# The buffers and transfers of the expert weights in a two-layer mixture-of-experts block

## What is computed

```python
D_MODEL, N_EXPERTS, TOP_K, EXPERT_DIM = 1024, 64, 8, 256

def _moe_routed(h, idx, wts, wg, wu, wd):
    ...
    def step(acc, blk):
        tok, w, e = blk
        xb = h_pad[tok]
        y = (jax.nn.silu(xb @ wg[e]) * (xb @ wu[e])) @ wd[e]
        return acc.at[tok].add(y * w[:, None].astype(y.dtype)), None
```

## Time and profile before

| | us |
|---|---|
| median of 3 runs | 3108.76 |
| lowest and highest | 3108.38, 3108.87 |
| the profiled execution | 3109.16 |
| its span, first to last instruction | 3107.3 |

### The profile page before, as it was taken

How to read it: one execution, slowest core, us unless ns; L and a number is a source line. 1 busy time by engine, 2 the same in 40 slices (tenths; PEclk the granted TensorE clock), 3 DMA queues, 4 the chain that set the end, 5 groups by cost and what they waited for, 6 DMA issues and landing times. The chain is left out here.

```text
span 3107.3 us, 44283 instructions
## 1 busy us (share of the span) xinstructions
PE 2711.0 (87%) x13505; PEld 1375.2 (44%) x13506; DVE 1126.3 (36%) x3283; ACT 575.0 (19%) x1306; POOL 389.7 (13%) x312
## 2 busy tenths in 40 slices
PE   5998989896969999999997588999977988999894
PEld 3555655654523333333332275666643333333331
DVE  2443452523323333333332643451433322223223
ACT  2222331311001111111111331331210111111111
POOL 0000001001012222222221200001010212122121
PEclk7999999996989999999998799999978999999997
DMA  6111213014177998999994502102134899998993
GB/s 250 55 72 41 84 40 120 14 42 175 48 288 237 363 324 266 317 310 325 328 354 128 200 1 85 68 28 107 35 146 188 336 371 379 365 390 283 380 329 100
DMA packets 109039, 619.21 MB, mean 199 GB/s; under 512 B 22800, under 2 KB 27152, under 8 KB 69264
## 3 DMA queue, kind: packets, MB, share of 16 engines
q1 hardware_dynamic: 75248, 530.30, 43.7%
q0 software_dynamic: 33696, 87.63, 11.6%
HBM read 578.84 MB, written 77.99 MB: 211 GB/s over the span
## 5 line engine op out<-in xcount | busy, mean ns | idle before, releaser
L1439 PE MATMUL ps<-wgu,xT 128*64 128x512 f32 x3584 | 820.2, 611 | 62.2 <-DMA wgu<-in_exp_gu 54.2
L1439 PEld LDWEIGHTS ps<-wgu,xT 128*64 128x64 f32 x3584 | 258.8, 140 | 529.0 <-issue 527.1
L1449 PE MATMUL ps<-wd,hiddenT 128*64 128x512 f32 x1824 | 421.2, 604 | 12.6 <-issue 11.5
L530 PE MATMUL ps<-w_in,hT 128*128 128x512 f32 (+3 forms) x1152 | 385.2, 493 | 14.5 <-PEq L484 3.8
L1375 POOL DMA_INDIRECT ffn_rows<-Y,six x114 | 182.5, 1601 | 1162.9 <-issue 779.0
L1598 DVE TENSOR_TENSOR hidden<-silu,ps 128x256 f32<-128x256 f32 x112 | 47.2, 421 | 737.0 <-ACT silu L1538 737.0
L530 PEld LDWEIGHTS ps<-w_in,hT 128*128 128x128 f32 x1152 | 205.2, 195 | 190.2 <-issue 183.2
L1449 PEld LDWEIGHTS ps<-wd,hiddenT 128*64 128x64 f32 x1824 | 128.3, 138 | 225.6 <-issue 225.6
L1538 ACT ACTIVATE silu<-ps 128x256 f32<-128x256 f32 x112 | 43.0, 384 | 831.6 <-PE ps L1439 831.6
L1592 DVE TENSOR_SCALAR Y<-ps,wc 128x512 f32<-128x512 f32 x114 | 85.6, 751 | 202.7 <-PE ps L1449 202.7
L1424 PE MATMUL ps<-cst,X 128*128 128x128 f32 x912 | 126.3, 282 | 34.9 <-DMA X<-h_rows,gix 19.1
(11 more groups left out here) (455 smaller groups left out, 2898.7 us busy)
## 6 DMA issues: line engine op xcount, KB each, us to landing
wgu<-in_exp_gu SPq DMA_DIRECT2D x128, 2048.0 KB, 13.1
wd<-in_exp_d SPq DMA_DIRECT2D x128, 1024.0 KB, 10.9
ada_start<-in_ada_w SPq DMA_DIRECT2D x8, 1024.0 KB, 13.2
w_in<-in_w_in SPq DMA_DIRECT2D x4, 2048.0 KB, 9.8
w_in<-in_w_out SPq DMA_DIRECT2D x4, 2048.0 KB, 11.9
aw_0A<-in_ada_w SPq DMA_DIRECT2D x6, 1024.0 KB, 4.8
aw_0B<-in_ada_w SPq DMA_DIRECT2D x6, 1024.0 KB, 5.0
aw_0C<-in_ada_w SPq DMA_DIRECT2D x6, 1024.0 KB, 4.8
```

What stands on the lines that cost most here:

```text
L530: last = pe.matmul(pp[i % 2][:, c0:c1], hT[:, k, i * P:(i + 1) * P], wg[g % 2][:, k, c0:c1], start=(k == 0), stop=(k == KD - 1))
L1439: last = pe.matmul(ps[h * HB:(h + 1) * HB, 0, :], xT[:, k, h * HB:(h + 1) * HB], wgu[w[h]][:, k, :], start=(k == 0), stop=(k == KD - 1))
L1449: last = pe.matmul(ps[h * HB:(h + 1) * HB, 1 + c, :], G[:, f, h * HB:(h + 1) * HB], wd[w[h]][:, f, c * 512:(c + 1) * 512], start=(f == 0), ...
```

## The change

The two tiles of a buffer become one, `wexp`, of 128 x 6144 numbers (3 MB); `wgu` and `wd` are now views into it. The weights lie in memory accordingly, the gate, up and down weights of an expert side by side (`exp_w`, made on the host before the launch, as the two arrays were). An expert is loaded with one transfer of 3 MB, which raises one semaphore, `weights_landed`; the gate/up and the down products both wait for it. SP's loop is one loop over the experts 4 to 63, with one wait each, on the count of down products. The products, their order and the passes stay as they are. The diff, cut to its core:

```diff
-        self.wgu = [sb(f"wgu0_{l}", [P, KD, 2 * FD], scope=scope)]
-        self.wd = [sb(f"wd0_{l}", [P, 2, D], scope=scope)]
+        self.w = [sb(f"wexp0_{l}", [P, KD * 2 * FD + 2 * D], scope=scope)]
...
-    eng.dma_start(ex.wgu[e][:, :, :].rearrange("p k n -> p (k n)"), v.t["exp_gu"][l, e]).then_inc(v.S(f"gate_up_landed{e}_{l}").sem, 16)
-    eng.dma_start(ex.wd[e][:, :, :].rearrange("p k n -> p (k n)"), v.t["exp_d"][l, e]).then_inc(v.S(f"down_landed{e}_{l}").sem, 16)
+    eng.dma_start(ex.w[e][:, :], v.t["exp_w"][l, e]).then_inc(v.S(f"weights_landed{e}_{l}").sem, 16)
...
-                def load_gate_up(w, e, free):
-                    sp.wait_ge(gate_up, free + CREDIT)
...
-                def load_down(w, e, free):
-                    sp.wait_ge(down, free + CREDIT)
...
-                with sp.Fori(0, E // NB - 2) as group:
+                with sp.Fori(1, E // NB) as group:
                     for w in range(NB):
-                        e = group * NB + (NB + 1 + w)
-                        load_gate_up((w + 1) % NB, e, free_after(e))
-                        load_down(w, e - 1, free_after(e - 1))
...
+                        e = group * NB + w
+                        free = sp.value_load(table[0:1, bass.ds(e + T_FREE, 1)], min_val=0, max_val=pairs)
+
+                        sp.wait_ge(down, free + CREDIT)
+                        sp.dma_start(ex.w[w][:, :], v.t["exp_w"][l][bass.ds(e, 1)].rearrange("a p n -> (a p) n")).then_inc(w_landed[w], 16)
...
-                        pe.wait_ge(w_gu[w[h]], landed[h])
+                        pe.wait_ge(w_landed[w[h]], landed[h])
...
-                        pe.wait_ge(w_d[w[h]], landed[h])
+                        pe.wait_ge(w_landed[w[h]], landed[h])
```

More of the change, by code:

```diff
@@ L1281, in sem @@
         return S(f"{n}_{l}").sem
-    w_gu, w_d = [sem(f"gate_up_landed{w}") for w in range(NB)], [sem(f"down_landed{w}") for w in range(NB)]
+    w_landed = [sem(f"weights_landed{w}") for w in range(NB)]
     listed, indexed, index, gathered = sem("slots_marked"), sem("slots_summed"), sem("index_ready"), [sem("gathered0"), sem("gathered1")]
@@ L1297, in experts @@
         for w in range(1, NB):
-            ex.wgu.append(sb(f"wgu{w}", [P, KD, 2 * FD]))
-            ex.wd.append(sb(f"wd{w}", [P, 2, D]))
-        wgu, wd, X, Y = ex.wgu, ex.wd, ex.X, ex.Y
+            ex.w.append(sb(f"wexp{w}", [P, KD * 2 * FD + 2 * D]))
+        X, Y = ex.X, ex.Y
+        wgu = [w[:, 0:KD * 2 * FD].rearrange("p (k n) -> p k n", k=KD) for w in ex.w]
+        wd = [w[:, KD * 2 * FD:].rearrange("p (k n) -> p k n", k=2) for w in ex.w]
         SG, HID, G = sb("silu", [P, FD]), sb("hidden", [P, FD]), sb("hiddenT", [P, 2, P])
@@ L1331, in _ @@
             def _(sp):
-                def load_gate_up(w, e, free):
-                    sp.wait_ge(gate_up, free + CREDIT)
-                    sp.dma_start(wgu[w][:, :, :].rearrange("p k n -> p (k n)"),
-                                 v.t["exp_gu"][l][bass.ds(e, 1)].rearrange("a p n -> (a p) n")).then_inc(w_gu[w], 16)
-                def load_down(w, e, free):
-                    sp.wait_ge(down, free + CREDIT)
-                    sp.dma_start(wd[w][:, :, :].rearrange("p k n -> p (k n)"),
-                                 v.t["exp_d"][l][bass.ds(e, 1)].rearrange("a p n -> (a p) n")).then_inc(w_d[w], 16)
@@ L1342, in free_after @@
-                def free_after(e):
-                    return sp.value_load(table[0:1, bass.ds(e + T_FREE, 1)], min_val=0, max_val=pairs)
                 for e in range(1, NB):
                     load_expert(v, sp, l, e, ex)
-                sp.wait_ge(gate_up, free_after(NB) + CREDIT)
-                sp.dma_start(wgu[0][:, :, :].rearrange("p k n -> p (k n)"), v.t["exp_gu"][l, NB]).then_inc(w_gu[0], 16)
-                with sp.Fori(0, E // NB - 2) as group:
+                with sp.Fori(1, E // NB) as group:
@@ L1359, in _ @@
-                sp.wait_ge(down, free_after(E - 1) + CREDIT)
-                sp.dma_start(wd[(E - 1) % NB][:, :, :].rearrange("p k n -> p (k n)"), v.t["exp_d"][l, E - 1]).then_inc(w_d[(E - 1) % NB], 16)
+                        e = group * NB + w
+                        free = sp.value_load(table[0:1, bass.ds(e + T_FREE, 1)], min_val=0, max_val=pairs)
+                        sp.wait_ge(down, free + CREDIT)
+                        sp.dma_start(ex.w[w][:, :], v.t["exp_w"][l][bass.ds(e, 1)].rearrange("a p n -> (a p) n")).then_inc(w_landed[w], 16)
@@ L1799, in layout @@
         "router_w": f["router_w"], "sh_g": f["sh_w_gate"], "sh_u": f["sh_w_up"], "sh_d": f["sh_w_down"],
-        "exp_gu": gu.reshape(L, E, P, KD * 2 * FD), "exp_d": ed.reshape(L, E, P, 2 * D),
+        "exp_w": np.concatenate([gu.reshape(L, E, P, KD * 2 * FD), ed.reshape(L, E, P, 2 * D)], axis=3),
     }
```

## The result

The changed kernel takes **3458.3 us** (median, 3454.9 to 3461.6) against 3108.8 before: 1.112 times the time, 95% interval 1.111 to 1.114. The forecast was 3480 with a range of 3400 to 3565. The profiled execution took 3454.9 us, span 3453.1, against 3109.2 and the earlier trace rows: +345.8 us of span, which is what follows by terms.

What follows compares the result with a forecast made beforehand. TensorE bounds the first expert loop, TensorE and the DMA queue in turns the second. Layer 1 stalls 342 + 8, layer 0 24 + 12, replaced waits -54, clock +40: 3109 + 372 = 3481, say 3480 us, range 3400 to 3565.

Steps and rivals of the forecast that it cites:

- table of distances: Both expert loops: passes from a buffer's last use to its next; distance 2 for 30 layer 1 reloads, 2 in layer 0.
- many waits under 1.5 us: First expert loop: perhaps many short TensorE waits for weights behind gate/up products, at reloads three passes apart.
- stall of distance 2: Gate/up products two passes after the buffer's last use: transfer fully exposed, landing 12.2 us, stall 12.0 us each.
- double ones: Five layer 1 passes needing two experts of distance 2: the second adds 8.4 us, 20.4 each.
- Pass 30: Layer 1: experts 43 and 44 leave behind one down and are both needed, 20.6 us against 12.4: 8 us.
- edge of distance 3 in layer 0: 24 layer 0 loads with 12.4 us from issue to need, against 12.2 to land: 0.5 us each, 12 together.
- waits that go: Second loop: the 12 existing waits for gate/up weights fall on passes that now stall longer and are replaced, -54 us.
- The clock: Gate/up products behind each stall run partly at 1.2 GHz, 2.1 us a stall over 28 stalls: +40 us.
- Waits for gathered rows: TensorE's waits for gathered rows may shrink as the queue is emptier: 0 to -10 us, taken 0.
- fewer, larger transfers feed the queue better: Rival: the DMA queue is the bound and one transfer per expert saves completions, so not slower: 3036 us; 2 in 100.
- The clock came back: Rival denied here: TensorE stays at 1.2 GHz in stalled passes, 12.5 us each in place of 2.1: 3760 us; 4 in 100.
- none took 16: Rival: the exposed transfer beside gather and scatter packets lands in 16 us, adding 180 us: 3660 us; 4 in 100.

Runs made afterwards that it cites:

- order_after: The changed kernel with experts reordered within groups of eight on the host, so 15 layer 1 reloads have distance 2 in place of 30: 3308.0 us.
- m5_after: The changed kernel with five weight buffers in place of four: 3235.4 us, 1.041 times the kernel before.
- late_two_both: The changed kernel without merging: two transfers of 2 and 1 MB, both released by the down count, gate/up products waiting for both: 3472.1 us.
- merged_8k: The changed kernel with 32 bytes of padding behind each 8 KB of a buffer row, cutting the 3 MB transfer into 8 KB pieces: 3502.9 us.

## Why the prediction was right

- **Where TensorE waits**: the table of distances named all 28 passes and no other; order_after and m5_after moved the waits as the table moves. Only the many waits under 1.5 us that layer 0 might have shown are absent, see the edge below.
- **A stall of distance 2**: forecast 12.0 us, from a landing of 12.2; measured 11.3 on average over the 22 single ones (10.7 to 12.0). The double ones: 20.4 forecast, 19.8 to 20.4 measured. Pass 30: 8 forecast, 7.8 measured. Together 374 forecast, 356 measured. The size was taken from the five quickest pairs of reloads in the trace; late_two_both shows what such a pair costs here, 13.5 us, and that the merged load is faster than it, 11.8. So 12.2 was too low for a pair, and that the merging would help the landing was left out of the sum. That the two nearly cancel is luck. The 9.2 us of the Trainium skill's fit (page DMA: Bandwidth & Descriptors, Anatomy of one DMA) is below every landing of 3 MB of weights in the changed kernel (10.7 us at the least).
- **The edge of distance 3 in layer 0**: forecast 12 us, measured 0. The term that was off is the landing again: 11.8 us is inside the 12.4 of cover. That the edge is there is shown by late_two_both and merged_8k, which land in 13.5 us and wait 17 times in layer 0, 15 of them at distance 3.
- **The waits that go**, -54, and down products that never wait for weights: as forecast.
- **The clock**: forecast +40, at 2.1 us a stall; measured +37. The gate/up products behind the 28 waits took 8.4 to 10.0 us, 9.1 on average, in place of 7.09.
- **Waits for gathered rows**: forecast 0 to -10, with 0 taken; measured +25. The step that failed is "may shrink as the queue is emptier": the queue is emptier on average, but the packets beside the gather's are longer, and merged_8k brings the waits back to 11.7. The quicker landing took 30 us off the forecast (18 in the stalls, 12 at the edge) and small waits of the kind "issue" another 14, for which the forecast had no term and no run shows a reason; the gathered rows put 25 on. That the sum stood within 22 us of the result owes something to luck, the 356 us of waits for weights do not.
- **The rivals**: "fewer, larger transfers feed the queue better" was right in kind and wrong in size: 14 us of 3472. It ends far from 3036, since at distance 2 the load is issued too late for the queue to matter: pass 2 waits for its own transfer from the issue on. The Trainium skill's advice to coalesce into one large transfer (the same page, Rules for kernel authors) is given there for many small transfers; here, with 1 and 2 MB, it was worth those 14 us. Its advice to issue early and wait late agrees with the 363 us that late_two_both costs. The clock came back behind each wait (the down products are busy 422.6 us in place of 421.2), and no wait for a single load was longer than 12.0 us, so none took 16.

## What to carry to other kernels

Before two buffers with different lifetimes are joined, write down for each load how long before its first use the slot comes free, with the real sizes of the work: the cost is not an average but sits on those uses whose slack falls below the time of one transfer. Here 32 of 120 reloads fell below it, and two more that were needed together; the later release and the joint wait cost 363 us, while the merging itself brought 14. If a landing time is near the slack (11.8 and 13.5 us against 12.4), small changes of a transfer's shape decide many small waits at once. And long packets are not free for a stream of small ones beside them: with five buffers the shorter rows were the faster kernel, with four the longer ones.

## What the runs showed of the hardware that was not expected

- A load's packets follow the length of the contiguous row in a partition: the packet records show whole rows of 24, 16 and 8 KB, at 0.92, 0.61 and 0.31 us each. Three megabytes landed in 11.8 us with rows of 24 KB and in 13.5 with rows of 8 KB or as 2 + 1 MB, beside the same gather and scatter.
- The small-packet stream on the other queue paid for it: TensorE's waits for gathered rows were 44 to 86 us with rows of 24 KB and 12 to 25 with shorter ones. In the wait of pass 2 the small-packet queue moved 0.29 MB beside 3.64 MB of weights with rows of 24 KB, and 0.58 beside 3.71 with rows of 8 KB. That the engines serve the two queues packet by packet is the reading of this, not a measurement.
